# Latent attention: scores of the first two groups in front of the second key and value unit

## The reference, cut to what matters

```python
def shared_latent_kv(h, positions, src_g, w_kv_a, kv_a_g, w_kv_b):
    ...
    kv = (c_kv @ w_kv_b).reshape(B, S, B_HEADS, QK_NOPE + V_HEAD)
    k_nope, v = kv[..., :QK_NOPE], kv[..., QK_NOPE:]
    k_pe = apply_rope(k_pe, rope_angles(positions))

def one_block(args):
    qn_b, qp_b, i = args
    s = (jnp.einsum('bqhd,bkhd->bhqk', qn_b, k_nope).astype(jnp.float32)
         + jnp.einsum('bqhd,bkd->bhqk', qp_b, k_pe).astype(jnp.float32)) * scale
    q_idx = i * Q_BLOCK + jnp.arange(Q_BLOCK)
    s = jnp.where(chunk_mask(q_idx, k_idx)[None, None], s, jnp.finfo(jnp.float32).min)
    p = jax.nn.softmax(s, axis=-1).astype(v.dtype)
    return jnp.einsum('bhqk,bkhd->bqhd', p, v)
```

## Time and profile before

| | |
|---|---|
| Time, median of 3 runs | 1063.13 us (1062.1 to 1063.21) |
| Time of the profiled execution | 1063.45 us |
| Its span, first to last instruction | 1061.6 us |
| PE busy | 1005.8 us, 95% of the span |
| DVE busy | 632.8 us, 60% |
| ACT busy | 484.3 us, 46% |
| Mean granted clock of TensorE | 0.974 of full speed |

### The profile page before, as it was taken

The page is one execution under the profiler, slowest core; times in us unless marked ns, Lnnn a source line. Parts: engine busy times, 40 slices in busy tenths (PEclk is TensorE's granted clock), DMA queues, the critical chain, the costliest instruction groups (busy, mean ns, idle before and its releaser), DMA issues.

```text
span 1061.6 us, 16624 instructions
## 1 busy us (share of the span) xinstructions
PE 1005.8 (95%) x6867; PEld 934.8 (88%) x6867; DVE 632.8 (60%) x748; ACT 484.3 (46%) x619; POOL 62.2 (6%) x63
## 2 busy tenths in 40 slices
PE   7989889889999999898999999999799999999997
PEld 7988778779999999898998899999699988999996
DVE  4377654467676676667555755555765755545554
ACT  5447522156455455542444544344445644444442
POOL 1000232020000000001000000000400000000000
PEclk9989979999999999999999999999999999999999
DMA  9733400046555555353555565556446236655640
GB/s 295 200 117 120 159 1 1 1 140 222 176 196 185 174 194 160 125 166 121 185 178 179 172 197 175 186 194 191 125 137 181 93 107 218 196 187 173 195 159 40
DMA packets 128591, 165.12 MB, mean 156 GB/s; under 512 B 20862, under 2 KB 111419, under 8 KB 128411
## 3 DMA queue, kind: packets, MB, share of 16 engines
q1 hardware_dynamic: 127067, 159.57, 46.8%
q0 software_dynamic: 1312, 4.74, 1.5%
q10 hardware_dynamic: 160, 0.07, 0.0%
HBM read 163.32 MB, written 1.05 MB: 155 GB/s over the span
## 4 chain that ended last, share of the span: by engine, by line
PE 84%; DVE 8%; ACT 4%; issue 2%; POOL 1%; DMA 0%; POOLq 0%; DVEq 0%; ACTq 0%
PE ps L224 26%; PE ps L225 25%; PE ps L226 25%; DVE w_lo L205 1%; ACT w_hi L197 1%; PE ps L990 1%; PE ps L1716 1%; PE ps L1710 1%; ACT act_tmp L339 1%; PE ps L1721 1%; DVE act_lo L649 1%; PE ps L1011 1%; PE ps L891 1%; ACT act_tmp L1040 1%; DVE union L1983 0%
## 5 line engine op out<-in xcount | busy, mean ns | idle before, releaser
L205 DVE TENSOR_TENSOR w_lo<-raw,w_hi 128x2048 fp32r<-128x2048 f32 (+1 forms) x152 | 343.3, 2263 | 167.8 <-ACT w_hi L197 166.8
L224 PE MATMUL ps<-hT_hi,w_hi 128*128 128x256 f32 x1192 | 341.2, 286 | 6.0 <-ACT act_tmp L623 3.7
L225 PE MATMUL ps<-hT_hi,w_lo 128*128 128x256 f32 x1192 | 339.2, 285 | 0.0
L226 PE MATMUL ps<-hT_lo,w_hi 128*128 128x256 f32 x1192 | 339.0, 284 | 0.0
L197 ACT ACTIVATE w_hi<-raw 128x2048 fp32r<-128x2048 f32 (+1 forms) x152 | 287.1, 1891 | 101.9 <-PE ps L226 93.8
L224 PEld LDWEIGHTS ps<-hT_hi,w_hi 128*128 128x128 f32 x1192 | 230.5, 193 | 8.9 <-issue 4.5
L225 PEld LDWEIGHTS ps<-hT_hi,w_lo 128*128 128x128 f32 x1192 | 230.6, 193 | 1.7
L226 PEld LDWEIGHTS ps<-hT_lo,w_hi 128*128 128x128 f32 x1192 | 230.6, 193 | 0.0
L224 PE MATMUL ps<-w_hi,act_hi 128*128 128x512 f32 x416 | 163.9, 394 | 5.5 <-DVE act_lo L649 5.5
L225 PE MATMUL ps<-w_hi,act_lo 128*128 128x512 f32 x416 | 163.4, 393 | 0.0
L226 PE MATMUL ps<-w_lo,act_hi 128*128 128x512 f32 x416 | 162.8, 391 | 0.0
(11 more groups left out here) (289 smaller groups left out, 945.9 us busy)
## 6 DMA issues: line engine op xcount, KB each, us to landing
raw<-in_mlp_w_dram SPq DMA_DIRECT2D x64, 1024.0 KB, 5.3
raw<-in_w_up_dram SPq DMA_DIRECT2D x22, 1024.0 KB, 5.0
raw<-in_a_w_in_dram SPq DMA_DIRECT2D x16, 1024.0 KB, 5.4
raw<-in_w_in_dram SPq DMA_DIRECT2D x12, 1024.0 KB, 5.8
raw<-in_w_down_dram SPq DMA_DIRECT2D x11, 1024.0 KB, 5.0
raw<-in_a_w_out_dram SPq DMA_DIRECT2D x8, 1024.0 KB, 4.9
raw<-in_w_out_dram SPq DMA_DIRECT2D x4, 1024.0 KB, 5.0
raw<-in_b_w_o_dram SPq DMA_DIRECT2D x4, 1024.0 KB, 5.0
```

Source lines behind the costliest of these rows:

```text
L205: nc.vector.tensor_tensor(w_lo[:, s, 0:n], raw[:, r, 0:n], w_hi[:, s, 0:n].bitcast(F32), ALU.subtract).then_inc(lo_ready, 1)
L224: nc.tensor.matmul(o, a[0], b[0], start=start, stop=False, skip_group_check=shared)
L225: nc.tensor.matmul(o, a[1], b[0], start=False, stop=False, skip_group_check=shared)
L226: return nc.tensor.matmul(o, a[0], b[1], start=False, stop=stop, skip_group_check=shared)
```

## The change

On PE the scores of groups 0 and 1 go between the second unit of queries and the second unit of keys and values, together with their two waits. On ACT the second values are taken out after the exponentials of both groups, and `split_hi(u0 + 9)` stays behind the values. On DVE the second keys are taken out after the maxima of both groups and the normalization of group 0, and `split_lo(u0 + 9)` goes behind them. Nothing is added or removed.

```diff
@@ mla_pe
             queries_pe(1, u0 + 5)
+
+            pe.wait_ge(m_qn, 2)
+            pe.wait_ge(m_rq, 2)
+            at_scores(pe, gs[0])
+            at_scores(pe, gs[1])
             pe.wait_ge(lo_ready, u0 + 7)
             pe.wait_ge(m_vev, 2)
             pe.wait_ge(m_ms, 2)
             pe.wait_ge(m_qn, 1)
             keys_values_pe(1, u0 + 6)
-
-            pe.wait_ge(m_qn, 2)
-            pe.wait_ge(m_rq, 2)
-            at_scores(pe, gs[0])
-            at_scores(pe, gs[1])
             pe.wait_ge(lo_ready, u0 + 8)
             pe.wait_ge(m_kev, 4)
             queries_pe(2, u0 + 7)
@@ mla_act
             split_hi(act, u0 + 8)
+            at_exp(act, gs[0])
+            at_exp(act, gs[1])
             values(1)
             split_hi(act, u0 + 9)
-            at_exp(act, gs[0])
-            at_exp(act, gs[1])
             at_copy(act, gs[0])
@@ mla_dve
             split_lo(dve, u0 + 8)
-            keys(1)
             dve.wait_ge(m_rs, 2)
             at_max(dve, gs[0])
-            split_lo(dve, u0 + 9)
             at_max(dve, gs[1])
             at_norm(dve, gs[0])
+            keys(1)
+            split_lo(dve, u0 + 9)
             rope(2)
```

## The result

The changed kernel takes 1067.02 us in the median of 20 runs, the kernel before 1062.82 us in 20 runs beside it. The medians are 4.20 us apart. The ratio is taken over all the runs and not from the two medians (the means are 1066.86 and 1063.40 us): it is 1.0033, with a 95% interval of 1.0017 to 1.0048, so the change is slower by 1.8 to 5.1 us. The forecast was 1066.3 us in a range of 1064.6 to 1068.2, with 0.82 on slower.

What follows compares the result with a forecast made beforehand. PE, busy in 95% of the span, was taken as the bound. Two waits and restarts, less a small gain, 1.47 + 0.05 + 1.63 + 0.08 - 0.05 = 3.18 us, on the median 1063.13 gave 1066.3 us, range 1064.6 to 1068.2.

Steps and rivals of the forecast that it cites:

- Wait 1: PE, in front of the moved scores: waits for DVE to finish the rotary queries, pushing PE by 1.47 us.
- Wait 2: PE, in front of queries 2: waits for DVE to take out the second keys, 1.63 us.
- restart: First PE matmul after a wait lasts longer: up to 0.08 us; 0.05 taken for the scores, 0.08 for queries 2.
- change of format: PE, first split-weight matmul after fp32 ones: its extra 0.18 us moves from queries 2 to the keys, sum unchanged.
- The turn in front of queries 3: PE's transposes of group 0: they no longer wait for the normalization, giving back under 0.1 us, taken as 0.05.
- rival D: DVE's queue holds the keys if softmax work runs over 1.8 us late; 1067.3 us at 1 us excess; chance 0.05.
- The split of u0+9: On ACT and DVE, later: DVE ends at about 831.1 instead of 824.50, hidden, just clear of rope(2) at 831.5.
- The wait of 1.03 us: PE's old wait at 853.40 for at_lo of group 2: moves along with PE and stays.
- Rival A: PE's clock also falls after the new waits: one fall costs 1.7 us more, time 1068.0; chance 0.14.
- rival B: The shift spares the clock fall at 879 us: 1.7 us comes back, time 1064.6; chance 0.14.
- main case: The two PE waits and nothing else: 1065.9 to 1066.8 us, chance 0.65.
- Rival C: Not slower: rope(1) and the copies take out part of the unit before it ends; 1062.0 us; chance 0.02.

Runs made afterwards that it cites:

- two half changes: Against the kernel before: only PE's list changed as in the change, 1072.89 us (ratio 1.0087); only ACT's and DVE's lists changed, 1068.61 us (ratio 1.0055).
- second comparison: The changed kernel, nothing edited, run again on another chip against the kernel before: 1067.48 us against 1064.13, ratio 1.0033.

## Why the prediction was right

**Wait 1** was forecast as a push of 1.47 us. Before, PE went on 0.20 us ahead of the start of `rope(1)`. Now `rope(1)` begins at 812.38 (L1392), so PE would have gone on at 812.38 - 0.20 = 812.18. It began the scores at 813.75: 1.57 us. The signal from L1395 took 0.15 us and not 0.05. I had taken the row with the same type of matmul as nearest; the other, 0.14, was right.

**Wait 2** was forecast as 1.63 us. In the same way, PE would have gone on at 824.88 - 0.20 = 824.68 and went on at 826.32: 1.64 us. The keys took 1.29, the signal 0.15.

**The small terms.** The scores took 5.13 us start to start (5.10 forecast, with a restart of 0.05 that came out as 0.08), keys and values 824.68 - 818.88 = 5.80 (5.81). The 0.18 us for the change of format moved as said: the first key matmul now lasts 0.47 us, and the first of queries 2, which had 0.47 before, 0.35. The restart of queries 2 was 0.07. The turn in front of queries 3 gave back 0.10 where 0.05 was forecast: from the first matmul of queries 2 to the first of queries 3 it is 831.06 - 826.32 = 4.74 us, before it was 828.56 - 823.61 = 4.95, and 0.11 of the difference is the change of format and the restart. Together: 1.57 + 0.08 + 1.64 + 0.07 - 0.10 = 3.26, against 3.18 forecast and 3.24 in the stretch.

**What costs nothing.** DVE had 2.60 us to spare in front of the keys, where I had left it 1.8 as a bound, so rival D did not happen. The split of u0+9 ended at 830.27, 0.63 us before `rope(2)`. The last load of the output weights was issued at 830.30 instead of 824.53, and no engine of the stage waited for it. The wait of 1.03 us stayed, 3.24 us later in the stage.

**The clock.** Rival A did not happen: the clock was 1.00 behind both new waits in all three profiles of the changed kernel. What the forecast had wrong was to read the fall at 879 as the fixed price of a wait of 1.84 us; it comes and goes in both kernels (below). The medians differ by 1067.02 - 1062.82 = 4.20 us in one comparison and by 1067.48 - 1064.13 = 3.35 in the other, around the same 3.24 us of the stretch. The Trainium skill (TensorE: Matmul & The Clock Gate, HAM oscillation) tells of a kernel in which PE waits for data longer than it works, and comes back at the half rate each time. Behind the longest waits of the two half changes, 3.06 and 4.40 us, the trace agrees (0.72 and 0.74). The new waits of 1.40 to 1.48 us are shorter and far apart, and none of them was followed by a fall.

**The base, and luck.** The forecast started from three runs that lay within 1.1 us, and held that closeness against rival B. The 20 runs of the kernel before go from 1060.95 to 1068.16 us. So the 0.7 us between the forecast and the median, which put the median 0.2 us above the main case's own range of 1065.9 to 1066.8, say nothing about the two waits, and that they are no more is in part luck. The forecast is borne out by the stretch: 3.24 us, forecast as 3.18 between 2.9 and 3.4. Rival B is not what the change did, as the 194.0 us behind the stage are the same in the first profiles of both kernels. But a last stage without the fall, as B had it, occurs in the third profile of the changed kernel and in the second of the kernel before (192.6 us in both), so with the change and without it.

Rival C, that part of the unit is taken out before it ends, is false for the kernel as written and true for the one with a semaphore of its own: that run is its proof, and it gives back just the one wait.

## What to carry to other kernels

Before you move work forward on the engine that sets the time, ask what it hid. Here 5.6 us of keys and values hid the taking out of one unit and 5.1 us of scores that of the next; swapped, each stood directly behind the unit it needs, and 1.2 and 1.3 us of DVE work came into the open, each with 0.35 us of start and signal, for a gain of 0.1 us, as PE had hardly waited for the softmax. If the order is wanted anyway, give the part that is waited for its own semaphore and put half a unit between. A hand-made order on one engine has to be moved with those of the others: in the stretch, half of this change costs more than the whole (8.0 and 5.9 us against 3.2).

## What was not expected of the hardware

**The same wait, with and without a fall of the clock.** Both kernels have a wait of 1.84 us for L623 at the start of the last stage. In two profiles of the changed kernel it ends at nearly the same time (882.75 and 882.76 us), and the clock in the 6 us from 883.4 is this in the second and this in the third profile:

```profile
883.40:889.40 6.00, 6.00 (x40) 6.00 (x39) 3.12 (x3) 1.51 (x2) 1.72 (x3) 0.72 1.03 354
```

```profile
883.40:889.40 6.00, 6.00 (x49) 5.87 (x48) 3.12 (x3) 2.14 (x4) 1.73 (x3) 1.00 0.93 334
```

In the 13 profiles of this study a fall came behind this wait in 8, behind the same wait near 592 us in 7, and behind the one of 2.36 us near 489 us in 7. They don't fall independently: the 7 profiles with a fall near 489 us are the 7 with one near 592 us. Each fall is worth 0.28 x 6 = 1.7 us by estimate, while the change is worth 3.2. That such falls make the scatter shows in the clocks of whole executions: of the 17 of the kernel before in the second comparison, the four with a mean granted clock of 0.977 or 0.978 took 1059.27 to 1063.50 us, and the seven with 0.971 or 0.972 took 1064.73 to 1068.82 us. The wait of 1.56 us near 211 us was never followed by one, nor were the 11 new ones of 1.40 to 1.48 us. Length is not the whole of it: the two waits of 1.41 and 1.47 us before 228.50 and 231.06 us, 2.6 us apart, were followed by a fall in all 13 profiles (0.74 in the kernel before), and so were the two like them near 426 and 429 us. The two new waits of the change end 12.6 us apart. That the distance is the reason was not tested. Why a fall comes in one execution and not in the next stays open. A stretch inside one stage, taken from the trace, repeats to 0.02 us where the whole time scatters by several.
